# New orders of V's products and low parts at the beginning, and x normed on VectorE before it is turned

## The reference, cut to what matters

```python
y = mixer_or_ffn(h)
x = x + gate[:, None, :] * rms_norm(y, g_post)      # gate: columns of c_act @ ada_w + ada_b
h = rms_norm(x, g_pre) * (1.0 + scale) + shift      # scale, shift: other such columns
```

## Time and profile before

| what | us |
|---|---|
| median of 3 runs | 1044.78 (1044.73 to 1045.03) |
| the profiled execution | 1045.76 |
| its span, first to last instruction | 1044.0 |
| TensorE busy | 1020.3 (98%) |
| VectorE busy | 785.7 (75%) |
| ScalarE busy | 538.5 (52%) |
| mean granted clock of TensorE | 0.996 of 2.4 GHz |

### The profile page before, as it was taken

How to read it: one execution, slowest core, us unless ns; L and a number is a source line. 1 busy time by engine, 2 the same in 40 slices (tenths; PEclk the granted TensorE clock), 3 DMA queues, 4 the chain that set the end, 5 groups by cost and what they waited for, 6 DMA issues and landing times.

```text
span 1044.0 us, 17276 instructions
## 1 busy us (share of the span) xinstructions
PE 1020.3 (98%) x7098; PEld 898.2 (86%) x7099; DVE 785.7 (75%) x1162; ACT 538.5 (52%) x706; POOL 74.8 (7%) x79
## 2 busy tenths in 40 slices
PE   6999999999999999999999999999999999999997
PEld 3677799889988999887989899899999689999995
DVE  2457798768878888866968778761787689878786
ACT  4443644344446457765545445454763565544543
POOL 0000000000000000000720000000790000000000
PEclk9999999999999999999999999999999999999999
DMA  9999699887997997003988777723344277555511
GB/s 339 384 369 353 220 348 357 316 318 279 336 330 258 277 376 287 1 5 125 390 300 314 273 285 281 228 86 117 122 141 158 67 249 235 168 196 185 179 41 41
DMA packets 131226, 243.56 MB, mean 233 GB/s; under 512 B 6521, under 2 KB 97228, under 8 KB 125004
## 3 DMA queue, kind: packets, MB, share of 16 engines
q1 hardware_dynamic: 126640, 238.77, 65.1%
q10 hardware_dynamic: 4507, 3.69, 1.3%
HBM read 239.30 MB, written 1.05 MB: 230 GB/s over the span
## 4 chain that ended last, share of the span: by engine, by line
PE 86%; DVE 6%; DMA 2%; ACT 2%; SPq 2%; issue 1%; DVEq 0%; ACTq 0%
PE bank L1898 24%; PE bank L1830 13%; PE bank L1832 12%; PE bank L1831 12%; PE bank L1910 3%; PE bank L1741 2%; DVE wlo L1135 2%; PE bank L1786 1%; SPq L607 1%; PE bank L2175 1%; DMA raw<-in_b_w_in_dram 1%; PE bank L2201 1%; DMA raw<-in_ada_w_dram 1%; PE bank L1768 1%; PE bank L1844 1%
## 5 line engine op out<-in xcount | busy, mean ns | idle before, releaser
L1135 DVE TENSOR_TENSOR wlo<-raw,whi 128x2048 fp32r<-128x2048 f32 (+1 forms) x145 | 331.5, 2291 | 60.0 <-ACT whi L674 58.4
L674 ACT ACTIVATE whi<-raw 128x2048 fp32r<-128x2048 f32 (+1 forms) x145 | 274.9, 1897 | 143.9 <-PE bank L1898 80.5
L1830 PE MATMUL bank<-hcat,whi 128*128 128x256 f32 x1096 | 313.2, 286 | 2.6 <-DVE wlo L1135 2.6
L1831 PE MATMUL bank<-hcat,whi 128*128 128x256 f32 x1096 | 310.7, 284 | 0.0
L1832 PE MATMUL bank<-hcat,wlo 128*128 128x256 f32 x1096 | 310.7, 284 | 0.0
L1830 PEld LDWEIGHTS bank<-hcat,whi 128*128 128x128 f32 x1096 | 209.7, 191 | 9.2 <-DVE wlo L1135 4.0
L1831 PEld LDWEIGHTS bank<-hcat,whi 128*128 128x128 f32 x1096 | 209.8, 191 | 1.4
L1832 PEld LDWEIGHTS bank<-hcat,wlo 128*128 128x128 f32 x1096 | 209.7, 191 | 0.0
L1699 DVE SCALAR_TENSOR_TENSOR cvt<-ut,vec,cvt 128x189 f32<-128x189 f32 (+2 forms) x176 | 68.2, 429 | 22.2 <-ACT cvt L1101 19.8
L1898 PE MATMUL bank<-whi,fhi 128*128 128x512 f32 x240 | 77.0, 402 | 0.0
L1898 PE MATMUL bank<-whi,flo 128*128 128x512 f32 x240 | 74.6, 392 | 0.0
(11 more groups left out here) (405 smaller groups left out, 1700.0 us busy)
## 6 DMA issues: line engine op xcount, KB each, us to landing
raw<-in_ada_w_dram SPq DMA_DIRECT2D x40, 1024.0 KB, 8.0
raw<-in_ff_w_in_dram SPq DMA_DIRECT2D x32, 1024.0 KB, 6.9
raw<-in_ff_w_out_dram SPq DMA_DIRECT2D x32, 1024.0 KB, 6.8
raw<-in_w_ada_dram SPq DMA_DIRECT2D x24, 1024.0 KB, 6.5
raw<-in_w_up_dram SPq DMA_DIRECT2D x22, 1024.0 KB, 5.1
raw<-in_w_in_dram SPq DMA_DIRECT2D x12, 1024.0 KB, 5.4
raw<-in_w_down_dram SPq DMA_DIRECT2D x11, 1024.0 KB, 5.9
raw<-in_ada_w_dram SPq DMA_DIRECT2D x16, 512.0 KB, 11.9
```

The source lines that it names most:

```text
L674: act.activation(whi[:, m % SPL, 0:w], raw[:, pl.nm[m] % RAW, 0:w], ACT.Copy).then_inc(s_hi, 1)
L1135: dve.tensor_tensor(wlo[:, m % SPL, 0:w], raw[:, pl.nm[m] % RAW, 0:w], whi[:, m % SPL, 0:w], ALU.subtract).then_inc(s_lo, 1)
L1830: pe.matmul(dst, wh[:, kt, n], ah[:, kt, :], start=kt == 0, stop=False)
L1831: pe.matmul(dst, wh[:, kt, n], al[:, kt, :], start=False, stop=False)
```

## The change

There are two parts.

**At the beginning.** `v_tile` issues, for each of the four k, `hh*wh` and `hl*wh` first, and the four `hh*wl` after them. Where the tile is the first with its chunk (j = 0 and 2, tile 0) TensorE waits at the start for the high part of the weights only, and for the low part before the `hh*wl`. On VectorE `splits(1)` and `splits(3)` are taken away, so that the low parts of chunks 0 and 1 come after `split_h` of the first four pieces, and those of chunks 2 and 3 after `split_h` of the last four; the low part of U's first chunk comes before the last two of the six `vectors`. The columns of `S0` are turned one k earlier in V's tile (k = 1 instead of 2).

**At the boundaries.** `norm_tile` no longer writes `xd`; it multiplies `x` by its norm in four pieces of 128 by 256 into `yg`, each with its own semaphore step. `x_transposes` waits for a piece, then turns its two 128 by 128 parts by the identity in TensorE's transpose form. `mods(between)` moves from behind tile 0's norm to between tile 1's `add` and the squares of its new `x`. The columns of `G1A`, `S1B` and `S2B` are no longer turned by TensorE between the two tiles of `y` but after `x_transposes(e, 0)` of the following boundary; for `G1A` and `S1B` they go to bank 6 instead of 7.

```
+    COL_BANKS = {G1A: 6, S1B: 6}
...
-    xd = sb("xd", [P, 2, P])
     onesm = sb("onesm", [P, P])
...
     s_yb, s_sqy, s_yg, s_x = sem("y_bank_complete"), sem("y_squares"), sem("y_times_gain"), sem("x_ready")
-    s_sqx, s_xd, s_xT = sem("x_squares"), sem("norm_diagonal"), sem("x_normed_and_transposed")
+    s_sqx, s_xd, s_xT = sem("x_squares"), sem("x_normed"), sem("x_normed_and_transposed")
     s_t, s_hh, s_h = sem("modulated"), sem("h_hi_ready"), sem("h_ready")
...
         if b in TWO_TILES:
-            return ps[ADA_BANK][:, 0:8].rearrange("p (n g) -> p g n", g=2)
-        return ps[ADA_BANK][:, 0:32].rearrange("p (n g c) -> p g n c", g=4, c=2)[:, :, :, c]
+            return ps[COL_BANKS.get(b, ADA_BANK)][:, 0:8].rearrange("p (n g) -> p g n", g=2)
+        return ps[COL_BANKS.get(b, ADA_BANK)][:, 0:32].rearrange("p (n g c) -> p g n c", g=4, c=2)[:, :, :, c]
...
                 r, q = rsqrt(ssx, tt)
-                if e:
-                    dve.wait_ge(s_xT, 4 * e)
-                dve.tensor_scalar(xd[:, tt, :], ident[:, :], r, q, ALU.mult, ALU.mult).then_inc(s_xd, 1)
+                for i in range(4):
+                    n = slice(T * i, T * i + T)
+                    dve.tensor_scalar(yg[:, tt, n], x[:, tt, n], r, q, ALU.mult, ALU.mult).then_inc(s_xd, 1)
...
                     add(2 * tt + 1)
+                    if tt and between is not None:
+                        mods(between)
                     if e is not None:
                         mods(late)
-                    if not tt and between is not None:
-                        mods(between)
...
             mods(S0X)
-            splits(1)
             split_h(0, hh, hl, range(4))
             mods(S0)
-            splits(3)
             split_h(0, hh, hl, range(4, 8))
             for n in range(2, 6):
+                if n == 4 and has("gmlp"):
+                    splits(M_U[0] + 1)
                 vectors(n)
...
-                if b:
+                if b - 1 in COL_BANKS:
+                    pe.wait_ge(s_row, b)
+                elif b:
                     pe.wait_ge(s_read, b)
...
                 for n in range(4):
-                    mm = pe.matmul(ps[ADA_BANK][:, w * n:w * n + w], stage[:, P * n:P * n + P], sel, start=True, stop=True)
+                    mm = pe.matmul(ps[COL_BANKS.get(b, ADA_BANK)][:, w * n:w * n + w], stage[:, P * n:P * n + P], sel, start=True, stop=True)
                 mm.then_inc(s_col, 1)
...
-                pe.wait_ge(s_xd, 2 * e + tt + 1)
                 for kt in kts:
+                    if kt % 2 == 0:
+                        pe.wait_ge(s_xd, 8 * e + 4 * tt + kt // 2 + 1)
                     c0 = T * (kt % 2) + P * tt
-                    mm = pe.matmul(ps[X_BANKS[kt // 2]][:, c0:c0 + P], x[:, tt, kt * P:kt * P + P], xd[:, tt, :],
-                                   start=True, stop=True)
+                    mm = pe.transpose(ps[X_BANKS[kt // 2]][:, c0:c0 + P], yg[:, tt, kt * P:kt * P + P], ident[:, :])
                     if tt and kt % 2:
...
                 boundary(2 * f + 1, meanwhile, first)
+                if f == 1:
+                    pe.wait_ge(s_read, S1B + 1)
                 ff_in(0, o=o)
...
                 at_ = lambda b: (lambda k, s: b[:, 15 % 3, T * k + s.start:T * k + s.stop])
-                end_of_y(m0 + 30, r14, (at_(fhi), at_(flo)), squares_ready, lambda: ada_cols(ends_at(f, 14)))
+                end_of_y(m0 + 30, r14, (at_(fhi), at_(flo)), squares_ready, lambda: None)
                 ada_chunks(FF_ADA[f][14])
...
                     kt = 4 * r + k
-                    if k == 2 and between is not None:
+                    if k == 1 and between is not None:
                         between()
                     pe.matmul(dst, hh[:, kt, t], wh[:, k, :], start=kt == 0, stop=False, skip_group_check=True)
-                    pe.matmul(dst, hh[:, kt, t], wl[:, k, :], start=False, stop=False, skip_group_check=True)
                     if ready:
                         pe.wait_ge(s_h, kt + 1)
-                    mm = pe.matmul(dst, hl[:, kt, t], wh[:, k, :], start=False, stop=kt == KT - 1, skip_group_check=True)
+                    pe.matmul(dst, hl[:, kt, t], wh[:, k, :], start=False, stop=False, skip_group_check=True)
+                if ready:
+                    split_ready(m)
+                for k in range(4):
+                    kt = 4 * r + k
+                    mm = pe.matmul(dst, hh[:, kt, t], wl[:, k, :], start=False, stop=kt == KT - 1, skip_group_check=True)
                 if tt:
...
                         ada_chunks(1)
-                    split_ready(M_V[j])
+                    if j in (0, 2):
+                        pe.wait_ge(s_hi, M_V[j] + 1)
+                    else:
+                        split_ready(M_V[j])
                     if j == 1:
...
             if has("attn"):
-                boundary(2, lambda e: ada_chunks(4))
+                def last_columns(b, u):
+                    pe.wait_ge(s_gain, 2 * u + 2)
+                    ada_cols(b)
+                    ada_chunks(4)
+                boundary(2, lambda e: last_columns(G1A, U_FF0))
+                pe.wait_ge(s_read, G1A + 1)
                 linear_mid(M_KC, gh, gl, o=2)
...
-                end_of_y(M_BO[2], h_rows(4), h_rows(6), last_heads, lambda: ada_cols(S1B))
+                end_of_y(M_BO[2], h_rows(4), h_rows(6), last_heads, lambda: None)
             if has("ffn1"):
-                ffn(1, 4, U_FF1, lambda e: ada_chunks(4))
+                ffn(1, 4, U_FF1, lambda e: last_columns(S1B, U_ATT))
                 x_transposes(4, 0)
+                ada_cols(S2B)
```

## The result

The changed kernel takes 1049.59 us (median of 5 runs, 1049.12 to 1052.45); the kernel before, on the same chip, 1044.80 (1044.73 to 1045.16). The ratio is 1.0049, 95% interval 1.0038 to 1.0061: 4.8 us slower. Forecast: 1047.6, 1043.0 to 1051.0.

The account below looks back on a forecast made before the run. TensorE, busy 98%, was taken as the bound, with a VectorE and ScalarE chain setting the boundaries' ends. From 1044.78 us: beginning -2.2, boundaries +2.0, clock +1.6 and +1.2, edge cases 0.2, giving 1047.6; 8-in-10 range 1043.0 to 1051.0.

Parts of the forecast that it names:

- Beginning, -2.2: V and U's first chunk: U's low part 0.5 us earlier, and half clock behind it avoided, 1.65: -2.2 us.
- VectorE's price: Norm on VectorE: a piece takes 412 ns, starts 0.33 us apart; each norm_tile costs 1.05 us more, twelve 12.6.
- Boundaries, +2.0: Boundary 1 +1.4 us, 2 and 3 about 0 each, 4 -0.3, 5 +0.9; together +2.0, bounds +0.8 to +3.0.
- The empty time: Boundary 1: TensorE, busy 7.41 of 7.80 us before, would be empty 3.8 us in 4.8, enough for a clock fall.
- Turning: TensorE at the boundaries: 96 records go, some 11 us of its time, but only -0.18 us a boundary on the path.
- Columns, 0: Between y's tiles at three stage ends: 0.8 us of TensorE records go, costed at nothing because VectorE is the limit.
- Clock, +2.8: TensorE's clock falls to 0.50 behind boundaries 1 and 5 after the new empty time: 1.6 and 1.2 us.
- The edge cases: Boundaries 2 and 3, TensorE empty 1.7 us in 2.6, at the edge of a fall; edge cases put in at 0.2 us.
- The first: Rival: the clock holds at the boundaries, leaving -2.2 + 2.0: 1044.6 us; chance 0.24.
- the faster one: Rival: y's second tile, not VectorE, is the limit at the boundaries: -5.3, 1039.5 us; chance 0.10.
- The third: Rival: new waits for low parts bring the clock down near 28 us, so the beginning does not pay: 1049.1; chance 0.16.
- The fourth: Rival: transposes count as idle for the clock, so it falls at each of boundaries 1 to 5: 1052.9 us; chance 0.07.

Follow-up runs that it names:

- e2: The kernel before with everything of the diff but the beginning's edits: 1050.11 us, ratio 1.0055.
- e3: The kernel before with only the norm in pieces on VectorE and the turns as transposes; columns and mods stay where they were: 1052.91 us, ratio 1.0079.
- e1: The kernel before with the beginning's edits alone: 1046.02 us, ratio 1.0008.
- e4: The kernel before with only the columns moved (other bank, inside the norm chains) and mods after the second tile's sums; xd and float32 turns stay: 1045.05 us.
- e6: The kernel after with boundary 1's late mods moved ahead of tile 1's pieces on VectorE: 1048.44 us, ratio 1.0033.
- the first four experiments: e1, e2, e3 and e4; the kernel before, run beside them on the same chip, had a median of 1044.75 us.
- e9: The kernel after with each transpose of the turns issued twice onto the same place: 1048.92 us, ratio 1.0041.
- e8: The kernel after with the turns as float32 products of the same pieces by the identity, two records each: 1049.62 us, ratio 1.0049.
- e5: The kernel before with the beginning's edits, and the first gate's mods ahead of the layer norm's large VectorE instructions: 1043.16 us, ratio 0.9986.
- e10: The kernel before with only the first gate's mods moved ahead of the layer norm's large VectorE instructions: 1043.65 us, ratio 0.9988.
- e12: e5 with boundary tile 0 by xd and float32 products, tile 1 by pieces and transposes, boundary 1's late mods behind tile 1's first piece: 1041.42 us, ratio 0.9966.

## Why the prediction was right, and where not

The direction and the range were right, the likeliest value 2.0 low. Step by step:

- **Beginning, -2.2: the step that failed.** The instructions up to U's second chunk were close to where they were put, and -2.17 is what the trace has at 63 to 80 us (0.70 of it at U's first chunk, where 0.5 was put in; 58.2 - 1.6 + 1.0 is 57.6, not 57.7). But I stopped there. The wait for the ada bank at 82 takes it back, behind a VectorE chain tied to transfers; I had looked for the next limit among U's low parts alone ("the second chunk of U has its low part at 64.7 ... so not more than 2.8 can be won") and not at the bank's. And three quarters of the term, the 1.65 for the half clock, were read from an execution that is not the median one. The 0.98 between the profiled execution and the median, which I took off as a constant, has the size of just this fall (1.05 at 95 us against e2 and e3); that it is the same one is not shown. Beside a median run of before the new beginning brings nothing (e1).
- **VectorE's price.** Pieces of 410 ns (412), 0.33 apart; 1.03 for tile 0 in boundary 1 (1.05). Right.
- **Boundaries, +2.0.** Boundary 1 +1.41 (+1.4), 2 +0.32 (0), 3 0.00 (0), 4 -0.27 (-0.3), 5 +0.81 (+0.9): +2.3. Right, but for a slip at 2 and 3: 1.05 - 0.39 - 0.37 is 0.29, not 0.2. Among the signs I wrote that the first product comes 3.8 after tile 1's first piece. The terms themselves give 1.68 and 1.11, 2.8, and the trace has 2.81; the sum did not use the slip. The empty time was put at 3.8 in 4.8 (2.4 ahead of the pieces, 0.3 among them, 1.1 behind), and the trace has 1.81, 0.3 and 0.93, 3.0 in 4.2.
- **Turning.** 96 records go, as forecast, but "some 11 us" of TensorE was too much: 24.6 less 96 x 0.15 is 10.2, and the trace has 16.7 for the turns, 7.9 less, a part of them at the half clock. It was in no sum.
- **Columns, 0.** Right, with the mechanism (e4: 0.9 earlier, 0.9 back).
- **Clock, +2.8.** Boundary 1: 1.6 forecast, 1.89 in the profiled run. Boundary 5: 1.2 forecast; none in after, one in e2 (1.4) and in e6 (1.2). The edge cases: one in boundary 3 (e3).
- **The sum for a median run.** The median span of after is 1047.4, that of before 1042.9 (beside the first four experiments): 4.5. The table has 0.6 for the beginning against the median before (-0.43 against -1.05), 2.3 for the boundaries, 1.9 for boundary 1's clock and -0.4 near 380: 4.4. It takes half clocks elsewhere as equal in both, which is not shown. Of the 4.8 between the medians, 0.4 lies outside the span (below).
- **Luck.** Against this sum the beginning was forecast 2.8 too good, and the clock, with 3.0 for all boundaries, 1.1 too dear. The two errors partly cancel; with the beginning alone put right, the forecast would have been 1050.4 and the miss 0.8 on the other side.
- **Rivals.** The first (the clock holds at the boundaries) and the faster one (the second tile is the limit) are out by after and e4. The third, that the beginning does not pay, named 1049.1 and is nearest in number; its mechanism, a clock fall near 28, did not happen. The fourth did not happen as stated; whether transposes have a part in the falls stays open.

## What to carry to other kernels

When a gain is forecast at one place, follow the engine on to its next wait of any kind, a bank's as well as data's, and to the clock on which the chain runs that frees it: here one instruction of 0.16 us, placed behind 6.5 us of work that nobody waited for, ate 1.7 of 2.2 us. Before a fall of TensorE's clock goes into a sum, see whether more than one execution has it. Splitting a step so that the next engine starts after its first piece paid here on the tile that ends the chain, and with unrelated work behind that first piece; on the other tile it cost 1.03.

## What the runs showed of the hardware

- The same gap of 1.6 us ahead of the same products was followed by a half clock in one trace of five with the old beginning. The kernels differ in placement, and also had half clocks far behind any edit, such as at the products of 33 rows near 720 to 726: eight of 14 traces fell there, and after's double one cost 3.0 us.
- A half-clock stretch of 3.4 us costs 1.4 to 1.6 us among dense products (1.46 at 497 and 1.47 at 726 in e3, 1.6 at 447.8 in before), 1.4 and 1.2 behind boundary 5 (e2, e6), and 0.3 where it falls on the turns, which wait for the pieces in any case (e9, boundary 1: 1.70 against 1.38 in e8).
- In boundary 1 TensorE stood idle ahead of tile 1's turns for 1.45 to 1.82 us in six traces, and each has a half clock there; in the other eight, for 0 to 1.36 us, and none has one.
- Time outside the span: 1.8 us (median) in the kernels with `xd` for both tiles at the start (before, e1, e4, e5, e10 to e12), 2.1 to 2.4 in those with pieces there (after, e2, e3, e6 to e9). 0.4 of the 4.8 us is thus in no stretch of the profile. Its cause was not looked for.
